# The samples' attention run inside the prompt's attention blocks

## The chip, the cores and the metric

The kernel runs on one core of a Trainium2 chip. The metric is the device time of one execution in microseconds (us). TensorE is called PE below, VectorE DVE, ScalarE ACT, GpSimdE POOL, and SyncE SP.

## What is computed

A two-layer decoder trunk runs one step for a prompt of 1024 tokens and for 8 samples of one token each. Both groups share the weights. Layer 0 has sparse attention with 8 heads of 64 and a retention mixer, layer 1 an SSD mixer, each followed by an MLP. The change concerns the sparse attention alone. An indexer has chosen up to 256 keys for each query. The prompt attends causally to its own keys; each sample attends to 1024 past keys and values, which lie in 8 pages of 128 rows found through a page table, and to its own new key and value:

```python
def sparse_attend(q, kg, vg, idx, tpos, rel_bias):
    dist = tpos[None, :, None] - idx
    bias = jnp.moveaxis(rel_bias[t5_bucket(dist)], -1, 2).astype(jnp.float32)
    logits = jnp.einsum('bqhd,bqkhd->bqhk', q, kg).astype(jnp.float32) * (DH_A ** -0.5) + bias
    logits = jnp.where((dist >= 0)[:, :, None, :], logits, -jnp.inf)
    p = jax.nn.softmax(logits, axis=-1).astype(vg.dtype)
    return jnp.einsum('bqhk,bqkhd->bqhd', p, vg)
```

Keys that were not chosen are masked by a large negative number instead of being gathered out, so that both kernels work on all keys. All of it is fp32.

## The kernel before

The program is a row of stages, each a block of five engine programs that begins when all engines have left the stage before. Inside a stage each engine runs its own list in the order written, and the lists meet through counting semaphores. Around the change the stages are these.

- `project_and_choose` projects to q, k, v and also picks keys for blocks 4 to 6 on DVE.
- `keys_and_values` (L1195) turns k and v into rows on PE, copies them on DVE and stores them from SP's queue. On the same queue a chain of three dependent transfers builds the bias tiles (L1219, L1223, L1226); the stores of k stand behind them.
- `attend` (L1279) is the prompt's attention: 8 blocks of 128 queries, 8 heads in each, 64 steps n in all. Block i sees i+1 tiles of 128 keys. For each step PE makes the logits (`dot`, L1343), turns the probabilities (`turn`, L1353) and multiplies them with the values (`weigh`, L1363). DVE adds mask and bias and takes the row's maximum (`logits`, L1405 to L1414), ACT takes the exponential (L1481) and copies the turned tiles out of PSUM (`copy_turned`, L1473), and POOL prepares the mask with the bias (L1329). PE's list interleaves steps: at an odd n it does the `dot` of n+1 and n+2 first, then `turn(n)`, then `weigh(n-1)`. DVE spends what is left up to block 6 on choosing the keys of block 7 (`choose`, L851 and L853), 64 instructions of 1024 elements spread evenly over the work. After each block its rows are divided by their sums (`rows`, L1423), turned on PE (`turn_rows`, L1372) and split into a high and a low part (`high` on ACT, `low` on DVE) for the output projection.
- `attend_samples` (L1492) follows. SP and POOL load 64 key pages of 256 KB. DVE multiplies each sample's 8 pages by the query that PE has spread over the partitions (L1617) and sums over each head (L1621). A softmax over all samples follows (L1625 to L1651), which goes several times between DVE, PE and ACT. ACT's list holds, ahead of its exponential (L1676), the issues of the value pages of six samples (L1528). PE then multiplies the probabilities, as an 8-column stationary side, with the value pages as moving side, 512 columns each (L1591).
- `retention` comes next.

An fp32 matmul with 128 contraction rows appears in the trace as two records, a transpose as one.

Of the kernel before, what the change touches and what calls it, by code (L numbers as in the profile page):

```python
# [7 lines left out]
F32 = mybir.dt.float32  # L8
F32R = mybir.dt.float32r
I32 = mybir.dt.int32  # L10
ALU = mybir.AluOpType
# [849 lines left out]

def indexer(B, norm):
# [332 lines left out]
def keys_and_values(B):  # L1195
# [17 lines left out]
    with nc.Block() as block:  # L1213
# [27 lines left out]

        @block.tensor
# [36 lines left out]
def attend(B):  # L1279
# [14 lines left out]
    left = B.take("scores_left_sb", [P, NBLK * P])  # L1294
    best = B.take("best_sb", [P, 8])
    s_choice, s_chosen = B.tally("choosing_step"), B.sem("block_chosen")
# [15 lines left out]
    with nc.Block() as block:  # L1312
        @block.gpsimd
# [20 lines left out]
        def _(pe):  # L1334
            def dot(n):
                i, h = seq[n]
                L = width(i)
                if n >= 2:
                    pe.wait_ge(s_log, n - 1)
                r = slice(64 * (h % 2), 64 * (h % 2) + 64)  # L1340
                for c in range(0, L, 512):
                    w = min(512, L - c)
                    ins = nc.tensor.matmul(B.psum[:, 2 * (n % 2) + c // 512, 0:w], B.qkv[r, h // 2, i * P:(i + 1) * P],  # L1343
                                           B.qkv[r, 4 + h // 2, c:c + w], start=True, stop=True)
                ins.then_inc(s_dot, 1)

            def turn(n):
                i, h = seq[n]
                pe.wait_ge(s_prob, n + 1)
                if n >= 1:  # L1350
                    pe.wait_ge(s_pt, n)
                for j in range(i + 1):
                    ins = nc.tensor.transpose(B.psum[:, 4 + j // 4, (j % 4) * P:(j % 4 + 1) * P],  # L1353
                                              logit[:, n % 2, j * P:(j + 1) * P], B.ident[:])
# [12 lines left out]
            def turn_rows(i):  # L1367
                pe.wait_ge(s_o, i + 1)
                if i >= 1:
                    pe.wait_ge(s_lo, i)  # L1370
                for j in range(4):
                    ins = nc.tensor.transpose(B.psum[:, 7, j * P:(j + 1) * P], o[:, j * P:(j + 1) * P], B.ident[:])  # L1372
                ins.then_inc(s_ot, 1)

            dot(0)
            dot(1)
            for n in range(N + 1):
                if n % 2 == 1 and n + 2 < N:
                    dot(n + 1)
                    dot(n + 2)  # L1380
# [4 lines left out]

                if n >= 1 and n % HA == 1 and n > 1:
                    turn_rows(n // HA - 1)
            turn_rows(NBLK - 1)

        @block.vector  # L1390
        def _(dve):
# [25 lines left out]
            def rows(i):  # L1417
                dve.wait_ge(s_pv, HA * (i + 1))
                dve.wait_ge(s_prob, HA * (i + 1))
                if i >= 1:  # L1420
                    dve.wait_ge(s_ot, i)
# [7 lines left out]
            def low(i):  # L1429
                dve.wait_ge(s_hi, i + 1)  # L1430
                out = B.hl[:, 0:4, i * P:(i + 1) * P]
                nc.vector.tensor_tensor(out, B.psum[:, 7, :].rearrange("p (k c) -> p k c", k=4),
                                        B.hh[:, 0:4, i * P:(i + 1) * P].bitcast(F32), ALU.subtract).then_inc(s_lo, 1)

            def choose(step):
                i = LATE + step // (2 * ROUNDS)
                choose_step(dve, s_choice, mask(i), left[:, 0:width(i)], best[:], step % (2 * ROUNDS))
                if step % (2 * ROUNDS) == 2 * ROUNDS - 1:
                    mark_left(dve, s_choice, mask(i), left[:, 0:width(i)])
# [7 lines left out]
            for n in range(N):  # L1447
                logits(n)
                work += width(seq[n][0])
# [5 lines left out]
                if n >= HA and n % HA == 3:  # L1455
                    low(n // HA - 1)
            rows(NBLK - 1)
            low(NBLK - 1)

        @block.scalar  # L1460
        def _(act):
            def high(i):
                act.wait_ge(s_ot, i + 1)
                nc.scalar.copy(B.hh[:, 0:4, i * P:(i + 1) * P],
                               B.psum[:, 7, :].rearrange("p (k c) -> p k c", k=4)).then_inc(s_hi, 1)
# [9 lines left out]
            for n in range(N):  # L1475
# [9 lines left out]
                if n >= HA and n % HA == 2:  # L1485
                    high(n // HA - 1)
            copy_turned(N - 1)
            high(NBLK - 1)
    B.top = mark


def attend_samples(B):  # L1492

    nc = B.nc
    mark = B.top
    KS, VS = 3, 3
    kp = B.take("k_pages_sb", [P, KS, PAGES, 512])
    vp = B.take("v_pages_sb", [P, VS, PAGES, 512])
    pick = B.take("pick_sb", [NS, NS, P])
    maskt = B.take("sample_mask_sb", [P, PAGES, NS])  # L1500
    logit = B.take("sample_logits_sb", [P, NS, PAGES, HA])
    own_prod = B.take("own_product_sb", [NS, 512])
    own = B.take("own_logit_sb", [NS, HA])
    owned = B.take("own_logit_diagonal_sb", [NS, NS, HA])
    pmax = B.take("page_max_sb", [P, NS * HA])
    hmax = B.take("head_max_sb", [NS * HA, 1])
    dmax = B.take("head_max_diagonal_sb", [NS * HA, NS * HA])
    pown = B.take("own_prob_sb", [P, NS * HA])
    pownd = B.take("own_prob_diagonal_sb", [NS, NS, HA])
    den = B.take("denominator_sb", [P, NS * HA])  # L1510
    att = B.take("sample_att_sb", [P, 4, NS])
    kept = pick[:].rearrange("p (s b) c -> p s (b c)", s=2)
    s_kept, s_col = B.sem("own_columns_kept"), B.sem("columns_summed")
    s_k, s_v = [B.sem(f"k_pages_{b}") for b in range(NS)], [B.sem(f"v_pages_{b}") for b in range(NS)]
    s_pick = B.sem("pick_loaded")
    (s_mt, s_q, s_prod, s_dots, s_ob, s_mxt, s_mb, s_sub, s_exp, s_sum, s_pvd, s_fin, s_hi, s_owned, s_pmax,
     s_dmax, s_pownd) = (B.sem(x) for x in (
         "mask_turned", "q_spread", "k_times_q", "dots", "own_spread", "max_turned", "max_spread", "max_subtracted",
         "sample_probs", "probs_summed", "sample_values", "sample_att", "sample_att_high",
         "own_logits", "page_max", "max_diagonal", "own_probs_diagonal"))  # L1520
    s_step = B.tally("sample_step")
    eye8 = B.ident[0:NS, 0:NS].unsqueeze(2).to_broadcast([NS, NS, HA])

    def load(eng, cache, place, b, sem):

        with eng.Fori(0, PAGES) as j:
            page = eng.value_load(B.pages[0:1, bass.ds(j + b * PAGES, 1)], min_val=0, max_val=NPOOL - 1)
            eng.dma_start(place[:, bass.ds(j, 1), :],  # L1528
                          B.i[cache][0][bass.ds(page, 1)].rearrange("o p h d -> p o (h d)")).then_inc(sem, 16)

    def load_keys(eng, parity):
        for b in range(parity, NS, 2):
            if b >= KS:
                eng.wait_ge(s_dots, b - KS + 1)
            load(eng, "cache_k", kp[:, b % KS], b, s_k[b])

    def key_place(b):

        return (NS - KS + b - VS) % KS

    def v_place(b):
        return vp[:, b] if b < VS else kp[:, key_place(b)] if b < VS + KS else vp[:, b - VS - KS]

    with nc.Block() as block:
        @block.sync
        def _(sp):
            sp.dma_start(pick[:].rearrange("p b c -> p (b c)"), B.i["pick"]).then_inc(s_pick, 16)
            load_keys(sp, 0)

        @block.gpsimd  # L1550
        def _(pool):
            load_keys(pool, 1)

        @block.tensor
        def _(pe):
            def to_columns(b):

                pe.wait_ge(s_kept, b + 1)
                for t in range(4):
                    ins = nc.tensor.matmul(B.psum[:, 7, b * 4 + t:b * 4 + t + 1], kept[:, b % 2, t * P:(t + 1) * P],  # L1560
                                           B.ones[0:HA, 0:1], start=True, stop=True)
                ins.then_inc(s_col, 1)

            for j in range(PAGES):
                ins = nc.tensor.transpose(B.psum[:, 0, j * NS:(j + 1) * NS], B.scores_s[:, j * P:(j + 1) * P],
                                          B.ident[0:NS, 0:NS])
            ins.then_inc(s_mt, 1)
            pe.wait_ge(s_pick, 16)
            for b in range(NS):
                if b >= 2:  # L1570
                    pe.wait_ge(s_prod, b - 1)
                nc.tensor.matmul(B.psum[:, 1 + b % 2, :], pick[:, b, :], B.qkv_s[:, 0, :], start=True, stop=True).then_inc(s_q, 1)
            pe.wait_ge(s_owned, 1)
            nc.tensor.matmul(B.psum[:, 3, 0:NS * HA], B.ones[0:NS, :], owned[:].rearrange("p b h -> p (b h)"),
                             start=True, stop=True).then_inc(s_ob, 1)
            pe.wait_ge(s_pmax, 2)
            nc.tensor.transpose(B.psum[0:NS * HA, 4, 0:P], pmax[:], B.ident[:]).then_inc(s_mxt, 1)
            pe.wait_ge(s_dmax, 1)
            nc.tensor.matmul(B.psum[:, 5, 0:NS * HA], B.ones[0:NS * HA, :], dmax[:], start=True, stop=True).then_inc(s_mb, 1)
            pe.wait_ge(s_exp, 2)  # L1580
# [1397 lines left out]
```

## Time and profile before

| | us |
|---|---|
| median of 3 runs | 3987.94 (3981.4 to 4002.66) |
| the profiled execution | 3990.57 |
| its span | 3989.0 |
| PE busy | 3445.2 (86%) |
| DVE busy | 1831.0 (46%) |
| ACT busy | 1086.6 (27%) |
| POOL busy | 1051.1 (26%) |

The span is the time from the first to the last instruction of the profiled execution. Busy time is a sum over the whole program, and a busy PE need not be a fast one: its records grow longer when its clock is lowered. The granted clock, as a share of 2.4 GHz, has two levels here, 1.00 and 0.50 (1.2 GHz); values between them are means over a stretch.

### The profile page before, as it was taken

Reading aid. Unit: us, or ns where it says so; the run is one execution under the profiler, and the core shown is the slowest. Engines: PE = TensorE matmul, PEld = TensorE weight load, DVE = VectorE, ACT = ScalarE, POOL = GpSimd, SP = SyncE. Lnnn points to the kernel's source line nnn. Section 1 sums busy time; section 2 is a strip of 40 time slices with the busy share of each in tenths; the row PEclk is TensorE's granted clock in tenths of the full one; section 3 lists DMA queues with packets and bytes.
Section 4 is the critical chain, followed back from the end, with each engine's and each line's share of the span. In section 5 each row is a group of like instructions: output and inputs, shape, how many; then the busy total and the mean of one; then the engine's idle time right before and its main releaser. Section 6 shows DMA issues by size and latency. Waiting matters only on the chain. (4 is left out here: it accounts for less than half of the span.)

```text
span 3989.0 us, 57770 instructions
## 1 busy us (share of the span) xinstructions
PE 3445.2 (86%) x20584; PEld 3168.3 (79%) x20584; DVE 1831.0 (46%) x3075; ACT 1086.6 (27%) x1873; POOL 1051.1 (26%) x737
## 2 busy tenths in 40 slices
PE   6889968737469999999959988898875999999998
PEld 5439966621359999999948888888865999999998
DVE  3699938761322221212136777777772121212122
ACT  3412204400133221213122444333433231213132
POOL 2002203210213222221124444445443332221222
PEclk8859987858779999999969999999987999999999
DMA  3011230063321111111122222222214111111111
GB/s 115 21 27 47 80 106 1 1 239 99 113 78 47 48 47 48 42 47 48 64 40 73 78 81 86 69 81 64 71 65 152 56 48 48 42 48 47 47 47 65
DMA packets 338555, 261.94 MB, mean 66 GB/s; under 512 B 51646, under 2 KB 307662, under 8 KB 336694
## 3 DMA queue, kind: packets, MB, share of 16 engines
q1 hardware_dynamic: 317174, 208.61, 17.4%
q10 hardware_dynamic: 11520, 25.24, 2.0%
q0 software_dynamic: 9728, 26.47, 1.9%
q8 instruction: 65, 1.06, 0.1%
q14 instruction: 68, 0.56, 0.0%
HBM read 217.36 MB, written 44.74 MB: 66 GB/s over the span
## 5 line engine op out<-in xcount | busy, mean ns | idle before, releaser
L228 POOL TENSOR_TENSOR w_low_sb<-w_loaded_sb,w_high_sb 128x1024 fp32r<-128x1024 f32 (+1 forms) x230 | 555.2, 2414 | 1936.1 <-ACT w_high_sb L222 1924.6
L245 PE MATMUL psum<-act_high_sb,w_high_sb 128*128 128x344 f32 (+1 forms) x2544 | 816.1, 321 | 30.9 <-PEq L186 17.2
L245 PE MATMUL psum<-act_low_sb,w_high_sb 128*128 128x344 f32 (+1 forms) x2544 | 814.4, 320 | 0.0
L245 PE MATMUL psum<-act_high_sb,w_low_sb 128*128 128x344 f32 (+1 forms) x2544 | 814.2, 320 | 0.0
L245 PE MATMUL psum<-second_high_sb,w_high_sb 128*128 128x344 f32 x1704 | 545.5, 320 | 0.0
L245 PE MATMUL psum<-second_low_sb,w_high_sb 128*128 128x344 f32 x1704 | 544.3, 319 | 0.0
L245 PE MATMUL psum<-second_high_sb,w_low_sb 128*128 128x344 f32 x1704 | 544.2, 319 | 0.0
L245 PEld LDWEIGHTS psum<-act_high_sb,w_high_sb 128*128 128x128 f32 (+1 forms) x2544 | 478.3, 188 | 32.6 <-issue 32.3
L245 PEld LDWEIGHTS psum<-act_high_sb,w_low_sb 128*128 128x128 f32 (+1 forms) x2544 | 478.6, 188 | 0.4
L245 PEld LDWEIGHTS psum<-act_low_sb,w_high_sb 128*128 128x128 f32 (+1 forms) x2544 | 478.4, 188 | 0.4
L222 ACT CAST w_high_sb<-w_loaded_sb 128x1024 fp32r<-128x1024 f32 (+1 forms) x230 | 239.5, 1042 | 650.5 <-PE psum L245 601.4
L2423 PE MATMUL psum<-act_high_sb,w_high_sb 128*128 128x344 f32 x1152 | 391.2, 340 | 11.5 <-POOL w_low_sb L228 11.4
L729 DVE TENSOR_TENSOR x_sb<-x_sb,psum 128x344 f32 (+1 forms) x192 | 98.5, 513 | 618.4 <-PE psum L245 618.4
L2423 PE MATMUL psum<-act_low_sb,w_high_sb 128*128 128x344 f32 x1152 | 373.2, 324 | 0.0
L2423 PE MATMUL psum<-act_high_sb,w_low_sb 128*128 128x344 f32 x1152 | 373.0, 324 | 0.0
L245 PEld LDWEIGHTS psum<-second_high_sb,w_low_sb 128*128 128x128 f32 x1704 | 320.3, 188 | 0.0
L245 PEld LDWEIGHTS psum<-second_low_sb,w_high_sb 128*128 128x128 f32 x1704 | 320.0, 188 | 0.0
L245 PEld LDWEIGHTS psum<-second_high_sb,w_high_sb 128*128 128x128 f32 x1704 | 320.0, 188 | 0.0
L2423 PEld LDWEIGHTS psum<-act_high_sb,w_high_sb 128*128 128x128 f32 x1152 | 222.4, 193 | 20.5 <-issue 9.9
L714 DVE SCALAR_TENSOR_TENSOR relu_sb<-psum,rstd_sb 128x344 f32<-128x344 f32 x192 | 99.2, 517 | 294.9 <-PE psum L245 270.8
L2423 PEld LDWEIGHTS psum<-act_low_sb,w_high_sb 128*128 128x128 f32 x1152 | 222.0, 193 | 2.9 <-issue 1.7
L2423 PEld LDWEIGHTS psum<-act_high_sb,w_low_sb 128*128 128x128 f32 x1152 | 221.2, 192 | 0.0
(414 smaller groups left out, 4789.5 us busy)
## 6 DMA issues: line engine op xcount, KB each, us to landing
w_loaded_sb<-in_w_up SPq DMA_DIRECT2D x64, 512.0 KB, 4.0
w_loaded_sb<-in_w_down SPq DMA_DIRECT2D x64, 512.0 KB, 3.6
w_loaded_sb<-in_w_in_odd SPq DMA_DIRECT2D x48, 512.0 KB, 3.9
ecay_sum_spread_sb<-decay_sum_scratch SPq DMA_DIRECT2D x8, 2048.0 KB, 9.7
w_loaded_sb<-in_w_in_even SPq DMA_DIRECT2D x28, 512.0 KB, 3.8
v_pages_sb<-in_cache_v ACTq DMA_DIRECT2D x40, 256.0 KB, 4.3
x_scratch<-x_sb SPq DMA_DIRECT2D x2, 4128.0 KB, 13.9
x_sb<-x_scratch SPq DMA_DIRECT2D x2, 4128.0 KB, 14.9
```

The source lines that it names most:

```text
L222: self.nc.scalar.copy(self.wh[:, par, :, 0:width], self.wf[:, par, :, 0:width]).then_inc(self.s_w_high, 1)
L228: self.nc.gpsimd.tensor_tensor(self.wl[:, par, :, 0:width], self.wf[:, par, :, 0:width], self.wh[:, par, :, 0:width].bitcast(F32), ALU.sub ...
L245: ins = nc.tensor.matmul(out, w[:, par, k, 0:width], a[:, k, cols], start=n == 0, stop=n == 3 * KT - 1)
L714: nc.vector.scalar_tensor_tensor(out=self.relu[:, s, :], in0=B.tile(self.par(e), t), scalar=0.0, in1=self.norm.rstd[:, tcols(t)], op0=ALU.max,
L729: nc.vector.tensor_tensor(xs, xs, B.tile(self.par(e), t), ALU.add).then_inc(B.s_tile_free, 1)
L2423: ins = nc.tensor.matmul(B.psum[:, t, 0:TT], w[:, par(e), k, :], a[:, k, tcols(t)], start=m == 0, stop=m == 3 * KT - 1)
```

## The change

`attend_samples` is removed as a stage. A class `Samples` takes its place and hands pieces of work to the four lists of `attend`, one piece after each step n.

- Page loads. All 128 pages (64 of keys, 64 of values) go through a ring of 7 groups of 4 pages. ACT issues the first 7 groups inside `keys_and_values`; SP issues the other 25 in `attend`, each when its place in the ring is free. POOL loads nothing more.
- Keys, steps 0 to 31 (blocks 0 to 3). In each step PE multiplies two turned key pages, as stationary side in four tiles of 128x128, with two columns that hold the query of one pair of heads, and turns the next two pages (four transposes each). ACT copies each turned page from PSUM.
- Softmax, steps 32 to 38, in small pieces on DVE, PE and ACT.
- Values, steps 38 to 63 without those with n mod 8 of 3 or 4 (20 steps). The value pages are the stationary side, in tiles of 128x128, and the probabilities of two heads the moving side, two columns. There are 32 units of 8 matmuls for the pages and one for the sample's own value.
- `turn_rows`, `high` and `low` are done in two halves at n mod 8 of 3 to 5, with half a PSUM bank, since the samples take the other half. Block 7's keys are chosen in place, without the scratch tile.

The core of the diff:

```diff
+        @block.scalar
+        def _(act):
+            for g in range(smp.RING):
+                smp.load(act, g)
...
+    GROUP = 4
+    RING = 7
+    MAX, SPREAD, SUM = 33, 34, 37
+    VALUES = [n for n in range(38, NBLK * HA) if n % HA not in (3, 4)]
...
+    def turn_pages(self, pe, m):
+        for p in (2 * m, 2 * m + 1):
+            if p % self.GROUP == 0:
+                self.await_group(pe, p // self.GROUP)
+            if p >= 2:
+                pe.wait_ge(self.s_kt, p - 1)
+            for t in range(4):
+                ins = nc.tensor.transpose(B.psum[:, 1 + 2 * (p % 2), t * P:(t + 1) * P], self.page(p)[:, t * P:(t + 1) * P], B.ident[:])
+            ins.then_inc(self.s_kturned, 1)
+    def dot_pages(self, pe, m):
+        for p in (2 * m, 2 * m + 1):
+            pe.wait_ge(self.s_kt, p + 1)
+            for t in range(4):
+                c0 = p * HA + 2 * t
+                ins = nc.tensor.matmul(B.psum[:, 5, c0:c0 + 2], self.kt[:, p % 3, t * P:(t + 1) * P],
+                                       self.qbd[:, t, p // PAGES, :], start=True, stop=True)
...
+    def step_pe(self, pe, n, s_lo):
+        if n < self.TURNS:
+            self.dot_pages(pe, n)
+        if n + 1 < self.TURNS:
+            self.turn_pages(pe, n + 1)
...
+    def weigh_values(self, pe, b, t):
+        out = B.psum[:, 7, c0:c0 + 2]
+        for j in range(PAGES):
+            nc.tensor.matmul(out, self.page(half * self.GROUP + b * PAGES + j)[:, t * P:(t + 1) * P],
+                             self.logit[:, b, j, 2 * t:2 * t + 2], start=j == 0, stop=False)
+        nc.tensor.matmul(out, B.qkv_s[:, 2, t * P:(t + 1) * P], self.pownd[:, b, 2 * t:2 * t + 2],
+                         start=False, stop=True).then_inc(self.s_value, 1)
...
+    def keep_turned(self, act, m):
+        for p in (2 * m, 2 * m + 1):
+            act.wait_ge(self.s_kturned, p + 1)
+            if p >= 3:
+                act.wait_ge(self.s_dots, p - 2)
+            self.B.nc.scalar.copy(self.kt[:, p % 3, :], self.B.psum[:, 1 + 2 * (p % 2), :]).then_inc(self.s_kt, 1)
...
+        @block.sync
+        def _(sp):
+            for g in range(smp.RING, smp.GROUPS):
+                smp.load(sp, g)
...
                 if n >= 1:
                     weigh(n - 1)
-
-                if n >= 1 and n % HA == 1 and n > 1:
-                    turn_rows(n // HA - 1)
-            turn_rows(NBLK - 1)
+                if n >= HA and n % HA in (3, 4):
+                    turn_rows(n // HA - 1, n % HA - 3)
+                if n < N:
+                    smp.step_pe(pe, n, s_lo)
...
-        keys_and_values(B)
-        attend(B)
-        B.top = B.even_top
-        attend_samples(B)
+        smp = Samples(B)
+        keys_and_values(B, smp)
+        attend(B, smp)
```

## Rows read from the trace of the kernel before

**Rows 1.** Page of the profile: granted TensorE clock, in tenths, in 40 slices.

```profile
PEclk8859987858779999999969999999987999999999
```

**Rows 2.** Windows (us from the start): blocks 0-3, block 4, blocks 5-7, samples.

```profile
core 0: us, PE busy (x) PEld busy (x) DVE busy (x) ACT busy (x) POOL busy (x), PEclk, DMA share, GB/s
595.00:661.00 66.00, 52.96 (x258) 39.58 (x259) 49.91 (x154) 28.47 (x89) 23.65 (x35) 0.67 0.00 1
661.00:697.00 36.00, 29.09 (x204) 23.42 (x203) 32.47 (x81) 16.22 (x34) 11.94 (x13) 0.95 0.00 1
697.00:818.00 121.00, 97.05 (x630) 79.14 (x628) 77.18 (x177) 49.00 (x77) 21.16 (x24) 0.86 0.00 1
818.00:1003.00 185.00, 92.63 (x239) 26.04 (x239) 84.75 (x49) 0.99 (x3) 17.43 (x32) 0.70 0.56 182
```

**Rows 3.** Timeline of DVE (start us, length us): last instructions of the two stages.

```profile
817.67 0.69 DVE L1432 TENSOR_TENSOR act_low_sb<-psum,act_high_sb 128x512 fp32r<-128x512 f32 x1 [1.37 <-ACT act_high_sb L1464]
...
1002.38 0.19 DVE L1667 TENSOR_TENSOR act_low_sb<-sample_att_sb,act_high_sb 128x32 fp32r<-128x32 f32 x1 [0.35 <-ACT act_high_sb L1683]
```

**Rows 4.** Groups (busy us, mean ns, idle) of 818 to 1003 us; its softmax window.

```profile
L1591 PE MATMUL psum<-v_pages_sb,sample_logits_sb 128*8 128x512 f32 x80 | 36.2, 606 | 0.0
...
L1617 DVE TENSOR_TENSOR k_pages_sb<-k_pages_sb,psum 128x4096 f32<-128x4096 f32 x8 | 35.3, 4413 | 14.1 <-DMA k_pages_sb<-in_cache_k 14.1
...
906.60:931.10 24.50, 4.81 (x8) 1.39 (x9) 5.91 (x15) 0.78 (x2) 0.00 (x0) 0.50 0.56 160
```

**Rows 5.** Timeline of PE in block 7, clock at 1.0 until 805.

```profile
795.97 1.06 PE L1353 MATMUL psum<-ident_sb,qkv_sb 128*128 128x128 f32 x8 [1.26 <-ACT qkv_sb L1473]
796.87 1.90 PE L1363 MATMUL psum<-v_rows_sb,qkv_sb 128*128 128x64 f32 x16
798.69 1.99 PE L1343 MATMUL psum<-qkv_sb 64*128 64x512 f32 x8
800.62 1.09 PE L1353 MATMUL psum<-ident_sb,qkv_sb 128*128 128x128 f32 x8
...
806.15 3.52 PE L1363 MATMUL psum<-v_rows_sb,qkv_sb 128*128 128x64 f32 x16
```

**Rows 6.** Windows of the line with 17 moving columns (L2137) alone.

```profile
2062.40:2064.70 2.30, 2.30 (x22) 2.30 (x22) 1.00 0.11 25
2064.80:2066.90 2.10, 2.10 (x12) 2.10 (x11) 0.50 0.14 29
```

**Rows 7.** Windows of PE around the one-column matmuls of L780 and L781.

```profile
3969.00:3972.00 3.00, 3.00 (x30) 1.00 0.00 0
3973.00:3974.00 1.00, 1.00 (x7) 0.50 0.00 0
```

**Rows 8.** Windows of PE while it only turns tiles (L1813, L1816).

```profile
1049.00:1054.00 5.00, 4.84 (x22) 0.50 0.00 0
1054.00:1055.00 1.00, 1.00 (x9) 0.80 0.00 0
```

**Rows 9.** Windows inside the attention: 594 to 614, 634 to 654, 660 to 714.

```profile
594.00:614.00 20.00, 14.61 (x61) 10.98 (x62) 12.14 (x45) 7.83 (x32) 8.57 (x16) 0.50 0.00 1
...
634.00:654.00 20.00, 18.33 (x70) 13.61 (x71) 13.67 (x40) 7.43 (x21) 5.98 (x8) 0.51 0.00 1
660.00:714.00 54.00, 42.45 (x304) 34.39 (x304) 49.80 (x121) 24.39 (x51) 15.25 (x18) 0.97 0.00 1
```

**Rows 10.** Groups of 590 to 818.5 us: copy of 128x512 by ACT.

```profile
L1464 ACT CAST act_high_sb<-psum 128x512 fp32r<-128x512 f32 x8 | 4.7, 586 | 6.5 <-PE psum L1372 6.4
```

**Rows 11.** Timeline of SP's and ACT's DMA issues.

```profile
558.57 0.61 SPq L1223 DMA_DIRECT2D bias_rows_scratch<-bias_scratch  x1
567.34 0.39 SPq L1226 DMA_DIRECT2D bias_sb<-bias_rows_scratch  x1
...
892.39 34.01 ACTq L1528 DMA_DIRECT2D k_pages_sb<-in_cache_v  x24
```

**Rows 12.** Window of the stage of the key and value rows.

```profile
552.00:595.00 43.00, 15.60 (x82) 12.29 (x82) 12.74 (x22) 0.00 (x0) 0.00 (x0) 0.67 0.49 162
```

More of the change, by code:

```diff
@@ L859, in mark_left, with choose_in_place @@
     tally.up(dve.scalar_tensor_tensor(out=S, in0=W, scalar=1.0, in1=S, op0=ALU.mult, op1=ALU.is_equal))
+def choose_in_place(dve, tally, S, m8, step):
+    if tally.count:
+        dve.wait_ge(tally.sem, tally.value())
+    tally.up(dve.max(m8, S) if step % 2 == 0 else dve.match_replace(S, m8, S, TAKEN))
 def indexer(B, norm):
@@ L1281, in attend @@
+def attend(B, smp):
     nc = B.nc
@@ L1365, in weigh, with turn_rows @@
                 ins.then_inc(s_pv, 1)
-            def turn_rows(i):
+            def turn_rows(i, half):
                 pe.wait_ge(s_o, i + 1)
[L1369 to L1372, printed above, removed]
+                if half == 1 or i >= 1:
+                    pe.wait_ge(s_lo, 2 * i + half)
+                if half == 0 and i == 0:
+                    pe.wait_ge(smp.s_own, 1)
+                if half == 0 and i == 3:
+                    pe.wait_ge(smp.s_sub, 1)
+                for j in range(2):
+                    c = slice((2 * half + j) * P, (2 * half + j + 1) * P)
+                    ins = nc.tensor.transpose(B.psum[:, 7, j * P:(j + 1) * P], o[:, c], B.ident[:])
                 ins.then_inc(s_ot, 1)
@@ L1376, in _ @@
             dot(1)
+            smp.begin_pe(pe)
             for n in range(N + 1):
-                if n % 2 == 1 and n + 2 < N:
-                    dot(n + 1)
-                    dot(n + 2)
+                if n % 2 == 1:
+                    for m in (n + 1, n + 2):
+                        if m < N:
+                            dot(m)
                 if n < N:
@@ L1454, in _, with high @@
                     rows(n // HA - 1)
-                if n >= HA and n % HA == 3:
-                    low(n // HA - 1)
+                if n >= HA and n % HA in (4, 5):
+                    low(n // HA - 1, n % HA - 4)
             rows(NBLK - 1)
-            low(NBLK - 1)
+            for half in range(2):
+                low(NBLK - 1, half)
+            smp.end_dve(dve)
         @block.scalar
         def _(act):
[L1462 to L1465, printed above, removed]
+            def high(i, half):
+                act.wait_ge(s_ot, 2 * i + half + 1)
+                nc.scalar.copy(B.hh[:, 2 * half:2 * half + 2, i * P:(i + 1) * P],
+                               B.psum[:, 7, 0:256].rearrange("p (k c) -> p k c", k=2)).then_inc(s_hi, 1)
             def copy_turned(n):
@@ L1684, in attend_samples @@
+            for half in range(2):
+                high(NBLK - 1, half)
+            smp.end_act(act)
     B.top = mark
```

399 lines of the change are left out of this document (212 added, 187 removed).

## The prediction

> **What bounds the kernel now.** I read the page's row of the granted clock first [rows 1], then cut the attention and the samples' stage into windows [rows 2]. Most of the kernel is dense matmul at the full clock and is not touched. The samples' stage is 185 us in which no engine works half the time: PE shows 93 us and DVE 85 us, one after the other. DVE's last instruction of the prompt's attention ends at 817.67 + 0.69 = 818.36 and its last of the samples' at 1002.38 + 0.19 = 1002.57 [rows 3], so the stage costs 184 us. Inside it DVE's multiplications of 4.41 us (and reductions as long) bound the keys, the softmax takes 24.5 us though DVE works 5.9 us in it, and PE streams 512 columns per value matmul [rows 4]. The prompt's attention is 223 us. In it PE is busy 80% of each window, and no engine is at its limit for long. Blocks 0 to 3 have a mean clock of 0.67, block 4 of 0.95, blocks 5 to 7 of 0.86 [rows 2].
>
> The question is therefore how much PE work the new form has, and at which clock it runs, since the attention has little idle PE time to hide it in: 66 - 53 = 13 us in blocks 0 to 3 and 121 - 97 = 24 us in blocks 5 to 7 [rows 2].
>
> **Prices on PE, full clock.** In block 7 the eight transposes of a step start at 795.97 and the next group at 796.87: 0.90 us, 0.11 each. The 16 records of `weigh` take 798.69 - 796.87 = 1.82 us, 0.114 each. Two `dot` of 1024 keys take 800.62 - 798.69 = 1.93 us. A step of the prompt with i+1 key tiles thus costs (0.90 + 1.82 + 0.97)/8 = 0.46 us per key tile [rows 5]. The added matmuls with 2 columns have no row of their own. The nearest is L2137, with 128-column weights and 17 moving columns: 22 records under way in 2.30 us, 0.11 each, while the clock is 1.00; 12 in 2.10 us, of which about two lie over the edges, hence 0.21 each, at 0.50 [rows 6]. So fewer columns do not make a record cheaper than 0.11, since the 64-column `weigh` costs the same, and at the low clock all of it doubles: `weigh` goes to 3.52 us for the same 16 records [rows 5].
>
> The Trainium skill, "TensorE: Matmul & The Clock Gate", section LDWEIGHTS, gives a weight load as its columns over 1.2 GHz, about 107 ns for 128 columns, and thus no doubling at the low clock. The 0.21 us above speak against it; by the page the half-clock price of every 2-column record would be halved.
>
> **The change part by part.** All sums are against the profiled execution (span 3989.0, time 3990.57).
>
> 1. Removed: the samples' stage, -184 us.
>
> 2. Keys beside blocks 0 to 3. 64 pages x (4 transposes x 0.11 + 4 matmuls x 2 records x 0.112) = 64 x 1.33 = 85 us on PE. The prompt's own steps are 8 x 0.46 x (1+2+3+4) = 37 us. Together 122 us at the full clock and 244 us at half. ACT copies 64 x 0.586 = 38 us [rows 10] beside its 28 us, far below either, and DVE keeps its 50 us. So PE becomes the bound in place of the exchange between the engines. PE waits in each step for the copy of the pages just turned (0.6 us each), but a step has its own `dot`, `turn` and `weigh` in between, about as long: nothing. The opening work on DVE (a dozen small operations) and three hand-offs in `turn_rows`, whose second half waits within the same step for ACT and DVE, I put at 5 us, together not more than 8.
>
> 3. The clock. In blocks 0 and 1 it was 0.50 for 20 us with PE busy 14.6 us, from 634 to 654 it was 0.51 with PE busy 18.3 of 20 us, and from 660 to 714 it was 0.97 with PE busy 42 of 54 us [rows 9]. So being busy as such does not decide it. The one-column matmuls of L780 and L781 ran back to back at 1.00 from 3969 to 3972, and at 3973 the clock was 0.50 with PE busy all the time [rows 7]; L2137 fell from 1.00 to 0.50 in the middle of its own run [rows 6]. Matmuls of few columns let the clock fall without any idle time. The new form puts 1.8 us of such matmuls into each of the steps 0 to 31 (16 records), and 28.8 records or 3.2 us into each of the 20 value steps. Against that, transposes alone raised the clock: 0.50 from 1049 to 1054, 0.80 in the next us [rows 8], and there are 8 more in each of the steps 0 to 31. I take for blocks 0 to 3 the mean clock that they had, 0.67, as transposes and small matmuls pull both ways: 122/0.67 = 182 us. With the 5 us it is 187 in place of 66: +121. The ends are 122 + 5 - 66 = +61 and 244 + 5 - 66 = +183.
>
> 4. Block 4 (36 us, DVE busy 32 of them [rows 2]). The moved softmax steps are 5.9 us of DVE [rows 4], and DVE is the bound here. For exchanges that now wait within a step I add 3 us. Two value steps add 2 x 3.2 us on PE, of which a part hides; at half clock they are twice that. I take 7. Sum +16, between +9 and +24.
>
> 5. Values beside blocks 5 to 7. 32 units x 9 matmuls x 2 records = 576 records x 0.112 = 64.5 us, of which 18 of 20 steps lie here: 58. The prompt's steps are 8 x 0.46 x (6+7+8) = 77. Together 135 us at full clock, 270 at half. The low stretches of 3.2 us come in three of four steps, nothing raises the clock but the prompt's own work, and the clock was already 0.86 here. I take six tenths of the work at the low level: 135 x 1.6 = 216 us, 3 for hand-offs, against 121: +98. The ends are 135 + 8 - 121 = +22 and 270 + 3 - 121 = +152.
>
> 6. Page loads in `keys_and_values`. 28 pages on ACT's queue, one every 34.01/24 = 1.42 us [rows 11], are 40 us of a stage of 43 us, and ACT is idle there. They move 7.3 MB. The samples' stage moved 182 GB/s at a DMA share of 0.56 [rows 2], 325 GB/s for all queues, so this is 22 us of DMA time in a stage that uses 0.49 of 43 us = 21 us [rows 12]. The sum just fits, but the stage is a chain on SP's queue: the rows of the bias tile take 567.34 - 558.57 = 8.8 us [rows 11], and the bias tile, the stores of k and DVE's copies wait behind them. Each transfer shares the engines with the pages. I take +8, between 0 and +22 (no overlap at all).
>
> 7. SP's 100 page issues in the attention need 100 x 1.42 = 142 us in a stage of over 300, nothing else stands on that queue, and a group is asked for 6 groups (12 steps) ahead: nothing. If that cover went, PE would wait at `await_group` with the turning. POOL loses its issues, which cost nothing. The end work on ACT and DVE: +1.
>
> Sum: -184 + 121 + 16 + 98 + 8 + 1 = +60, so a span of 4049 and a time of 4051. The median stands 2.6 us under the profiled execution: 4048.
>
> **Rivals.**
>
> - The clock holds at 1.00, as it did from 660 to 714 with PE busy 79% [rows 9], because PE is now never idle. Then the sum is -184 + 61 + 9 + 22 + 8 + 1 = -83, a time of 3905: clearly faster. It decides from a mean clock on: all that PE does in blocks 0 to 3 and 5 to 7 is 257 us at full clock, and the change breaks even if these blocks take 66 + 121 + 184 - 16 - 8 - 1 - 8 = 338 us, a mean clock of 0.76. For it speaks that PE's idle gaps go, against it [rows 6, 7]. Chance 0.18; values between it and the forecast are in its lower half.
> - The clock stays low nearly throughout. -184 + 183 + 24 + 152 + 8 + 1 = +184, a time of 4172. For it speaks that from 634 to 654 a busier PE than now did not get it back [rows 9]; against it the transposes [rows 8] and the two steps of each block without values. Chance 0.14.
> - Turning pages does not raise the clock, the rest as forecast: the blocks 0 to 3 are at +183 in place of +121, a time of 4110. [rows 8] speak against it, as nothing but transposes ran there. Chance 0.06. This is what the Trainium skill says in "TensorE: Matmul & The Clock Gate", Part 4, where the full clock "doesn't engage" for transposes; the row differs, and the measurement decides.
> - The transfers bind: pages and bias chain do not overlap, +22 in place of +8, and PE waits for the first groups. A time of 4062 to 4070. Speaks for it the DMA share of 0.9 and over while the bias rows move, against it the sum of item 6. Chance 0.10.
>
> **How the numbers follow.** The forecast, a mixed clock with the time near 4048, has 0.52; its own range, the mean clock of both parts between 0.72 and 0.58, is 4000 to 4100. A measurement of this kernel tells 0.5%, 20 us, from no change: under 3968 is faster, over 4008 slower. The first rival gives 0.18 faster, and the forecast's lower edge 0.02 more. Within 0.5% lie 0.10, from the forecast and the blend with the first rival. The rest, 0.70, is slower. For 8 in 10 the range reaches from 3940 to 4125: it leaves out the first rival's lower half (0.1) and most of the second (0.1).
>
> **What would show it.** In the profile after: the span from the first `logits` to `retention` near 450 us in place of 408; the granted clock of blocks 0 to 3 near 0.67 and of blocks 5 to 7 near 0.62; PE busy over 95% in both, with no engine waited for; 2-column matmuls 0.11 us apart at 1.00 and 0.21 at 0.50; block 4 near 52 us; `keys_and_values` longer by 8 us, its bias rows the longest link. The prediction is wrong if the clock stays at 1.00 through a value step, if PE waits for page copies or page loads, or if the 2-column matmuls are cheaper than the 17-column ones.

## The result and the profile after

| | before | changed |
|---|---|---|
| median, us | 3992.18 (3981.4 to 4002.66, 4 runs) | 4037.43 (4033.08 to 4049.86, 4 runs) |
| ratio to before | | 1.0113, 95% interval 1.0093 to 1.0134 |
| span of the profiled execution, us | 3989.0 | 4048.2 |

The change makes the kernel slower by 45 us; 4048 was forecast, within 3940 to 4125. The profiled execution of the changed kernel is the slowest of its four. One execution of all those in this study, of the form with 16 columns below, took 11795 us; the ratios leave it out, and the median of its other six is 4020.1.

The page's row of the granted clock answers to [rows 1]. A digit is a fortieth of the span, 101 us here. The seventh to the tenth, from 607 to 1012 us, read 5, 8, 5, 6; the same places of the kernel before, samples' stage and all, read 7, 8, 5, 8.

```profile
PEclk8869975856579999999979999999986999999999
```

The windows of the changed kernel answer to [rows 2, 12]. They are cut at the first logits of a block, and the first two windows of [rows 2] are not: at 661 us three of the eight logits of block 3 were still to come. The first logits with block 4's 384 far columns start at 670.00. So the kernel before has to be cut anew, first blocks 0 to 3, then block 4; blocks 5 to 7 are left with 120.3 us, up to 818.

```profile
595.00:671.00 76.00, 62.10 (x314) 46.35 (x315) 57.35 (x174) 32.33 (x98) 27.64 (x39) 0.69 0.00 1
671.00:697.70 26.70, 20.66 (x155) 17.36 (x155) 25.69 (x63) 12.37 (x25) 7.95 (x9) 1.00 0.01 1
```

Of the changed kernel these are the stage of the key and value rows, blocks 0 to 3, block 4, blocks 5 to 7 with the end of the stage. The columns are the time, then busy us and instructions of PE, of its weight loads, of DVE, ACT and POOL, then the clock, the DMA share and GB/s.

```profile
549.50:601.00 51.50, 17.63 (x82) 13.19 (x82) 13.08 (x22) 0.00 (x0) 0.00 (x0) 0.60 0.83 278
601.00:778.00 177.00, 174.52 (x1060) 158.42 (x1060) 60.83 (x187) 67.05 (x165) 27.66 (x39) 0.69 0.31 90
778.00:822.00 44.00, 39.16 (x199) 31.89 (x200) 31.47 (x75) 13.20 (x28) 7.93 (x9) 0.70 0.09 25
822.00:1053.00 231.00, 224.52 (x1191) 201.29 (x1191) 78.68 (x184) 50.01 (x82) 21.17 (x24) 0.63 0.15 42
```

Read the PE column against the time: 174.52 of 177 us and 224.52 of 231 us, at clocks of 0.69 and 0.63. PE is hardly ever free, and it runs at about two thirds of full speed. The 185 us of the samples' window are gone, and 238 us came back elsewhere: +101 in blocks 0 to 3 (177 against 76), +17 in block 4 (44 against 26.7), +111 from block 5 on (231 against 120.3), +8.9 in the stage of the key and value rows (51.5 against 42.6). The cuts are good to about a microsecond. That is +53 in all. Retention begins 50 us later than before, since the stage ahead began 3 us earlier. The rest of the span's difference lies in stages that the diff doesn't touch; from retention to the end they took between 2986 and 3009 us in the profiles of this study. For stretches I therefore use the time from the start of the key and value rows to the start of retention, called the three stages below: 450.6 us before, 503.5 us changed.

PE's waits, grouped by what ended them, from 549 to 1053 us (us in total, times, longest):

```profile
PE psum L1266 <- DVE k_rows_sb L1287: 22.8, 6, 17.5
PE psum L1635 <- PEq L1220: 9.1, 1, 9.1
...
PE psum L1647 <- ACT qkv_sb L1782: 4.7, 5, 2.1
PE psum L1671 <- DVE act_low_sb L1735: 2.6, 3, 1.0
...
PE psum L1635 <- ACT page_turned_sb L1454: 0.8, 1, 0.8
```

The first two belong to the stage ahead and its end. Inside the attention all waits together are some 11 us of 452; turned pages are waited for once, loaded pages never. So exchanges between the engines keep PE waiting for little of the attention, and transfers for none of it. The timeline of PE in two value steps shows what does (start, us, line, columns of the moving side, count):

```profile
902.04 1.81 PE L1441 MATMUL psum<-sample_logits_sb,w_high_sb 128*128 128x2 f32 x8
903.72 1.85 PE L1441 MATMUL psum<-sample_logits_sb,w_low_sb 128*128 128x2 f32 x8
...
916.52 1.00 PE L1441 MATMUL psum<-sample_logits_sb,w_high_sb 128*128 128x2 f32 x8
917.39 1.03 PE L1441 MATMUL psum<-sample_logits_sb,w_low_sb 128*128 128x2 f32 x8
```

Eight records of 2 columns take 903.72 - 902.04 = 1.68 us at the low clock, 0.21 each, and 917.39 - 916.52 = 0.87 us, 0.11 each, at the full one. The price that was taken from a 17-column line [rows 6] is that of 2 columns too.

### The profile page after: what moved, and what is told of

The parts are those of the page before. It is cut to its first block and busy times, and to the rows that moved or that the text cites. A ratio compares the mean times of both kernels' runs of the same rounds, so it can differ in the third digit from the quotient of the medians.

```text
span 4048.2 us, 60149 instructions
## 1 busy us (share of the span) xinstructions
PE 3619.8 (89%) x21704; PEld 3397.2 (84%) x21704; DVE 1758.8 (43%) x3063; ACT 1121.8 (28%) x1945; POOL 1036.3 (26%) x704
## 5 line engine op out<-in xcount | busy, mean ns | idle before, releaser
L245 PE MATMUL psum<-act_high_sb,w_high_sb 128*128 128x344 f32 (+1 forms) x2544 | 817.8, 321 | 31.7 <-PEq L186 17.2
```

The lines of the kernel that those rows point to most:

```text
L245: ins = nc.tensor.matmul(out, w[:, par, k, 0:width], a[:, k, cols], start=n == 0, stop=n == 3 * KT - 1)
```

## The experiments

The theory on record, A: the matmuls of 2 columns keep PE occupied and yet let the granted clock fall, and that is where the gain went. Its rival B: the number of records is what costs, and the clock is that of the prompt's own attention anyhow. Rival C: exchanges between the engines set the pace, and a busy PE is only the look of it.

### The same number of matmuls with wider moving sides

The edit gives each page matmul more columns. The key matmuls of the last 16 pages get fewer than 128, since the PSUM bank ends (`min(128, 512 - c0)`). The extra columns multiply data that happens to stand beside, and their products are written over by later matmuls or never read.

```diff
-        self.logit = B.take("sample_logits_sb", [P, NS, PAGES, HA])
+        self.flat = B.take("sample_logits_sb", [P, NS * PAGES * HA + 128])
+        self.logit = self.flat[:, 0:NS * PAGES * HA].rearrange("p (b g h) -> p b g h", b=NS, g=PAGES)
...
-        c0 = 448 + b * HA + 2 * t
-        out = B.psum[:, 7, c0:c0 + 2]
+        c0 = 320 + b * HA + 2 * t
+        out = B.psum[:, 7, c0:c0 + 128]
         for j in range(PAGES):
+            o = (b * PAGES + j) * HA + 2 * t
             nc.tensor.matmul(out, self.page(half * self.GROUP + b * PAGES + j)[:, t * P:(t + 1) * P],
-                             self.logit[:, b, j, 2 * t:2 * t + 2], start=j == 0, stop=False)
+                             self.flat[:, o:o + 128], start=j == 0, stop=False)
...
-                ins = nc.tensor.matmul(B.psum[:, 5, c0:c0 + 2], self.kt[:, p % 3, t * P:(t + 1) * P],
-                                       self.qbd[:, t, p // PAGES, :], start=True, stop=True)
+                w, o = min(128, 512 - c0), (t * NS + p // PAGES) * 2
+                ins = nc.tensor.matmul(B.psum[:, 5, c0:c0 + w], self.kt[:, p % 3, t * P:(t + 1) * P],
+                                       self.qflat[:, o:o + w], start=True, stop=True)
```

Both sides:

> The edit: every page matmul of the samples (keys and values) gets 128 moving columns in place of 2; the 126 extra columns are overwritten by later matmuls or never read, so the count of records stays 512 + 512. Theory A (the narrow matmuls let the granted clock fall, and the low clock is what the attention stage pays): a record of 128 moving columns costs about what a 2-column one costs at the full clock (0.11 us, as the transposes of 128 columns), the clock stays near 1.00, blocks 0 to 3 fall from 177 to 122-135 us, block 4 from 44 to 38-42, blocks 5 to 7 from 230 to 135-150: the kernel near 3905 (3885 to 3935), faster than both. Theory B (the time is set by the number of records, and the low clock belongs to the prompt's own attention, whose clock was 0.67 and 0.86 before): blocks 0 to 3 stay at 170-180 us, 5 to 7 at 220-240, the kernel at 4030 to 4060. Theory C (exchanges between the engines pace it, PE only looks busy): clock up, but the stretches stay above 165 and 215 us.

Keys alone:

> The edit: 128 moving columns for the key pages alone (steps 0 to 31), values as in the changed kernel. A: blocks 0 to 3 at 122-135 us with a clock over 0.9, blocks 5 to 7 unchanged at 230: 3990 (3980 to 4000), no longer told from the kernel before. B: 4030 to 4050.

Values alone:

> The edit: 128 moving columns for the value pages alone (steps 38 to 63), keys as in the changed kernel. A: blocks 5 to 7 at 135-150 us with a clock over 0.9, blocks 0 to 3 unchanged at 177: 3952 (3940 to 3970). B: 4030 to 4050.

The control with 16 columns:

> The edit: 16 moving columns for keys and values, a control: it changes the same lines as the 128-column form and writes extra columns too, but the matmuls stay narrow. A: the clock of the two stretches stays within 0.05 of the changed kernel's (0.69 and 0.63), the kernel at 4037 within 15 us. If it is as fast as the 128-column form, something else in the edit (the order of writes, the place of the results) makes the gain, and A falls. B: 4037 too.

| | median, us | ratio to before, 95% | blocks 0-3, us (clock) | block 4 | blocks 5-7 |
|---|---|---|---|---|---|
| changed, 2 columns | 4037.4 | 1.0113 (1.0093 to 1.0134) | 177 (0.69) | 44 (0.70) | 231 (0.63) |
| 128, keys and values | 3926.6 | 0.9828 (0.9803 to 0.9852) | 133 (0.98) | 40 (0.66) | 157 (0.99) |
| 128, keys alone | 4000.6 | 1.0015 (1.0000 to 1.0031) | 134.5 (0.97) | 41.5 (0.63) | 233.5 (0.62) |
| 128, values alone | 3978.9 | 0.9949 (0.9929 to 0.9969) | 173 (0.72) | 40.5 (0.66) | 157 (0.99) |
| 16, keys and values | 4024.8 | 1.0083 (1.0047 to 1.0118) | 153 (0.82) | 41.7 (0.63) | 230 (0.63) |

Windows of the form with 128 columns for both (blocks 0 to 3, block 4, blocks 5 to 7), and of the control with 16 (the same three):

```profile
601.80:735.00 133.20, 130.05 (x1074) 118.85 (x1075) 61.77 (x191) 65.28 (x165) 27.74 (x39) 0.98 0.40 121
735.00:775.00 40.00, 38.05 (x197) 31.70 (x197) 32.11 (x77) 13.28 (x28) 7.99 (x10) 0.66 0.07 21
775.00:932.30 157.30, 149.75 (x1180) 132.39 (x1179) 77.39 (x180) 50.03 (x82) 21.20 (x24) 0.99 0.21 61
```

```profile
602.00:755.00 153.00, 150.28 (x1072) 136.86 (x1072) 61.86 (x192) 66.09 (x165) 27.66 (x39) 0.82 0.37 107
755.00:796.70 41.70, 39.82 (x196) 32.60 (x195) 31.82 (x77) 13.27 (x28) 7.94 (x9) 0.63 0.05 16
796.70:1027.00 230.30, 223.78 (x1184) 200.23 (x1183) 77.61 (x180) 50.31 (x82) 21.16 (x24) 0.63 0.14 42
```

The count of PE's records is the same in every row of the table but for records missing from the traces (1074, 1072 and 1060 in blocks 0 to 3), and so are pages, copies, waits and transfers. With up to 64 times the columns in each page matmul the kernel is 111 us shorter than the changed one, and 1.7% under the kernel before. Each half of the edit acts only in its own stretch, 177 to 134.5 and 231 to 157 (the other half's stretch stays at 173 and 233.5), and the shares add up: the three stages are 503.5 us (changed), 463.5 (keys), 423 (values) and 383 (both), which is -40, -80 and -121. B is refuted, and C too: the exchanges are there as before.

Three expectations were clearly off, and the keys alone came out just above their range (4000.6, 3980 to 4000). Blocks 5 to 7 took 157 us, where A gave 135 to 150. A value unit (eight page matmuls and the own value, 18 records) takes 2.25 us at the full clock, 0.125 per record with its two small ones, as the timeline of that form shows, where 18 x 0.112 = 2.0 was reckoned; 31 of the 32 units lie in this stretch, and not 28.8; and waits, the turned rows and the end of the stage come on top.

```profile
809.01 1.11 PE L1445 MATMUL psum<-sample_logits_sb,act_low_sb 128*128 128x128 f32 x8
809.96 1.06 PE L1445 MATMUL psum<-sample_logits_sb,w_loaded_sb 128*128 128x128 f32 x8
810.95 0.38 PE L1447 MATMUL psum<-wn_prob_diagonal_sb,sample_qkv_rows_sb 8*128 8x2 f32 x2
811.26 0.87 PE L1652 MATMUL psum<-ident_sb,qkv_sb 128*128 128x128 f32 x6
```

The values alone gave 3979, not 3952: its three stages are 80 us shorter than the changed kernel's (423 against 503.5), but its untouched stages were the longest of all in that profile (3009 us, 13 more than in the changed kernel's). Why they were is not shown; its ten executions spread from 3957 to 3989. And the control with 16 columns is not neutral: in blocks 0 to 3, where 8 transposes of 128 columns stand between the narrow matmuls, the clock rose from 0.69 to 0.82; in blocks 5 to 7 it stayed at 0.63. Its kernel time can't be told from the changed kernel's (the intervals overlap). The gain thus does not come from the new place of the results, which the control has too, and it depends on the columns by degrees.

### Idle matmuls in the kernel before

The smallest test has nothing of the change in it: at the head of steps 0 to 31 of the kernel before stand 8 matmuls whose products nobody reads, of 2 columns or of 128.

```diff
             for n in range(N + 1):
+                if n < 4 * HA:
+                    for _ in range(8):
+                        nc.tensor.matmul(B.psum[:, 5, 0:2], B.ident[:], B.ident[:, 0:2], start=True, stop=True)
                 if n % 2 == 1 and n + 2 < N:
```

> The kernel before with nothing of the change in it but 8 idle matmuls of 2 moving columns (16 records, into a PSUM bank that is free there) at the head of each of the steps 0 to 31: the smallest test of the clock without pages, copies, transfers or waits. PE's own work in blocks 0 to 3 is 37 us at the full clock, the idle matmuls add 512 x 0.112 = 57, together 94. Theory A (narrow matmuls let the clock fall): a clock of 0.50 to 0.65 and 145 to 190 us in place of 76 (first product to the first logits of block 4), the kernel 70 to 110 us slower than before. Theory B (only the number of records counts, the clock stays at what the prompt's own work had, 0.70): 115 to 135 us, the kernel 40 to 60 us slower.

> The same with 128 moving columns in the idle matmuls. A: the clock rises above 0.9 and the stretch takes 94 to 110 us, 20 to 35 us over before, and 40 us or more below the narrow twin, though each matmul does 64 times the work. B: the same time as the narrow twin or longer.

Measured: 4092.3 us with 2 columns (ratio 1.0233, 1.0203 to 1.0262) and 4020.3 with 128 (1.0057, 1.0032 to 1.0083). Windows from the first product to the first logits of block 4, the narrow form first:

```profile
591.70:764.60 172.90, 172.90 (x822) 158.37 (x823) 57.88 (x175) 33.41 (x98) 27.61 (x39) 0.53 0.00 1
```

```profile
592.50:693.70 101.20, 101.20 (x828) 91.57 (x828) 57.69 (x176) 32.24 (x98) 27.62 (x39) 0.98 0.00 1
```

In the kernel before this stretch is 76 us. By the profile PE is busy for the whole of both windows, with the same records. 172.9 x 0.53 = 92 and 101.2 x 0.98 = 99: the same work, at two clocks (94 had been reckoned). Here there are no pages, no copies and no transfers, so the fall of the clock belongs to the narrow matmuls themselves. The Trainium skill ("TensorE: Matmul & The Clock Gate", section "HAM oscillation — how this bites in real kernels") has as its rule that gaps in PE's work are what brings the clock down. In the narrow form the profile shows no gap at all, and the clock is 0.53. By that rule it would have been 1.00, and the stretch 92 us long, 80 us shorter, by an estimate from the window above. For PE's distance from its limit the Trainium skill ("Perfetto Trace Analysis", section "Identifying the Most-Contended Engine") gives two measures, the floating point work against the peak and the busy share of the weight loads. The second doesn't show the loss here: weight loads are busy 158.37 of 172.9 us, 92%, at about half the pace that PE could have. The clock beside it does.

This pair also bears on the prediction's third rival, by which turning pages does not raise the clock. The narrow form has 16 narrow records per step and no pages to turn, and its clock is 0.53; the changed kernel has as many with 8 transposes beside them, and its clock is 0.69.

### Fewer records

> Leaves out three of four key matmuls of each page (only the last pair of heads has logits) and seven of eight page matmuls of each value unit; transposes, copies, transfers and softmax steps stay. Records fall by 384 in blocks 0 to 3 and by 448 from step 38 on, at the full clock 43 and 50 us, at the low clock twice that. A: blocks 0 to 3 at 90 to 115 us (79 at full clock), blocks 5 to 7 at 120 to 145 (as in the kernel before plus the hand-offs), the kernel near 3870 (3840 to 3900). C (exchanges pace it): still over 150 and 190 us.

```diff
-            for t in range(4):
+            for t in (3,):
                 c0 = p * HA + 2 * t
...
-        for j in range(PAGES):
+        for j in range(1):
             nc.tensor.matmul(out, self.page(half * self.GROUP + b * PAGES + j)[:, t * P:(t + 1) * P],
```

3877.9 us (0.9697, 0.9667 to 0.9727). Its windows of blocks 0 to 3 and 5 to 7:

```profile
605.30:711.00 105.70, 100.12 (x705) 86.37 (x706) 61.46 (x191) 65.12 (x165) 27.68 (x39) 0.85 0.54 153
...
749.40:890.60 141.20, 125.69 (x750) 106.70 (x749) 77.17 (x180) 49.64 (x82) 21.16 (x24) 0.76 0.24 68
```

Without three quarters of the key matmuls and seven eighths of the page matmuls for the values, and with all turns, copies, softmax steps and transfers kept, 177 us become 106 and 231 become 141. C is out once more. It also shows how little the full count costs at the full clock: blocks 5 to 7 took 157 us with all matmuls at 128 columns, 16 us more than here without 448 of the records.

### The page loads ahead of the attention

```diff
-            for g in range(smp.RING):
+            for g in range(2):
                 smp.load(act, g)
...
-            for g in range(smp.RING, smp.GROUPS):
+            for g in range(2, smp.GROUPS):
                 smp.load(sp, g)
```

> The changed kernel, but ACT issues only 2 of the 7 page groups in the stage of the key and value rows; SP issues the other 5 at the head of the attention. If the page transfers are what lengthened that stage by 9 us (51.6 against 42.7), it is back at 43 to 46 us, and the attention, whose PE is never kept waiting for a page group, stays at 452 us: 4030 (4022 to 4036). If it was something else (a slower clock in that stage, the turns on PE), it stays at 51 us. If SP then falls behind in the first steps, PE waits at the first groups and the attention grows by 3 us or more.

The stage of the key and value rows took 46.1 us in place of 51.5. The kernel's time didn't move, where 4030 had been expected: 4039.6 us, ratio 1.0108 (1.0083 to 1.0132), with an interval wider than the 5 us in question. SP's issues in the stage, the changed kernel first, then this one, then the stores of k in the kernel before, name the place:

```profile
556.40 0.62 SPq L1230 DMA_DIRECT2D bias_rows_scratch<-bias_scratch  x1
564.78 0.39 SPq L1233 DMA_DIRECT2D bias_sb<-bias_rows_scratch  x1
565.22 21.70 SPq L1238 DMA_DIRECT2D out_k_prompt<-k_rows_sb  x8
```

```profile
555.37 0.61 SPq L1230 DMA_DIRECT2D bias_rows_scratch<-bias_scratch  x1
564.62 0.39 SPq L1233 DMA_DIRECT2D bias_sb<-bias_rows_scratch  x1
565.05 15.27 SPq L1238 DMA_DIRECT2D out_k_prompt<-k_rows_sb  x8
```

```profile
567.77 13.72 SPq L1231 DMA_DIRECT2D out_k_prompt<-k_rows_sb  x8
```

The bias rows take 8.4 and 9.3 us here against 8.8 before [rows 11]: the 7.3 MB of pages don't hold them up. It is the eight stores of k behind them that stretch, from 13.72 us before and 15.27 here to 21.70 us with all the pages under way. DVE, whose copies need the buffers that these stores free, waits for them 17.2 us before, 19.6 here and 25.4 in the changed kernel.

### The low clock of block 4

At 128 columns one low stretch was left, around block 4. Three forms add idle matmuls of 128 columns there: in step 31 alone, the same with the late page loads, and in steps 31 to 33 with the late loads. The second part of the diff is in the last alone (and in the form with 64 columns below):

```diff
+            if m == self.TURNS - 1:
+                for _ in range(8 // 2):
+                    nc.tensor.matmul(B.psum[:, 7, 256:384], B.ident[:], B.ident[:], start=True, stop=True)
             ins.then_inc(self.s_dots, 1)
...
+        if n in (self.TURNS, self.MAX):
+            for _ in range(8):
+                nc.tensor.matmul(B.psum[:, 7, 256:384], B.ident[:], B.ident[:], start=True, stop=True)
```

> The 128-column form had the low clock from about 737 to 765 us, at the entry of block 4: step 31 has key matmuls cut to 62 columns and less (the bank ends), no pages to turn after them, and PE waits 0.95 us for the scaled page logits. Here 8 idle matmuls of 128 columns stand among those of step 31 (+16 records, 1.8 us). If a short stretch of narrow work is what drops the clock, and the prompt's own steps then can't raise it for 28 us: the clock stays at 1.00 through block 4, which falls from 39.6 to 25-32 us, the kernel 6 to 12 us below the 128-column form: 3917 (3912 to 3922). If the clock falls anyway (block 4's own work is too thin after the wait), it is 1 to 3 us slower: 3928.

> The same with only 2 of the 7 page groups loaded in the stage of the key and value rows. The stage at 43 to 46 us in place of 52, the rest as its twin: another -5 to -9 us, near 3910. The steps are shorter here (4 us against 5.5), so SP's 1.4 us per page is closer to what two pages per step need (2.8 us): if PE waits for page groups in blocks 0 to 3, the gain is lost.

> With idle matmuls in step 31 alone the clock fell all the same, 6 us later (about 743 us), behind a wait of 1.89 us for DVE in step 32, and came back at 764. Here steps 32 and 33 have 8 idle matmuls of 128 columns each as well (16 records, 1.8 us, each). If the thin PE work of these steps is what drops the clock, it stays at 1.00 through block 4, which goes from 40 to 28-34 us: the kernel at 3912 (3907 to 3916), against 3921 for its twin. If it falls at another step of block 4, or DVE's softmax steps set the pace of block 4 whatever the clock is, the stretch stays at 38-42 us: 3921 to 3925.

Block 4 of the form with one filled step, then of that with three:

```profile
728.90:768.90 40.00, 36.90 (x210) 31.42 (x209) 31.69 (x74) 13.27 (x28) 7.95 (x9) 0.74 0.07 21
```

```profile
730.60:770.40 39.80, 36.77 (x241) 30.90 (x241) 31.63 (x74) 13.20 (x28) 7.95 (x9) 0.87 0.07 21
```

The key matmuls of step 31 have 16 columns and fewer, not the 62 of the expectation. The clock of block 4 went from 0.66 over 0.74 to 0.87, and the block took 40 us each time. The expected 6 to 12 us did not come. DVE is busy 32 of the 40 us in all of them, and its waits for results of PE are most of the rest: 6.7 us in the plain form, 7.1 with three filled steps. The fill is not free either: PE has 241 records there in place of 197, stays busy for 37 us, and part of the fill stands ahead of results that DVE waits for. So a clock raised by idle matmuls bought nothing here. What a higher clock would bring without them is not shown by these forms. The kernel before gives a hint: its block 4, without any idle matmuls, took 28.4 us at a clock of 0.79 behind the narrow ones of blocks 0 to 3, and 26.6 us at 1.00 behind the wide ones. The medians: 3925.8 us with one filled step, 3921.0 with the late loads besides (0.9822, 0.9799 to 0.9845; near 3910 was expected), 3922.2 with three filled steps (0.9814, 0.9801 to 0.9828). Between these and the plain form with 128 columns nothing can be told at the kernel's level; in the profiles the three stages are 383 us (plain), 383, 377 and 378, so the late loads keep their 5 us and PE never waits for a page there either.

> The same with 64 moving columns in the samples' matmuls (the idle ones keep 128). A record of 64 costs what one of 2 or of 128 costs at the full clock (0.11 us). The question is whether 64 columns keep the clock up as the prompt's own matmuls of 64 columns among wider ones do. If they keep it, the time is its twin's within 5 us. If each fall of the clock is now slower to mend, or 64 are too few, blocks 0 to 3 and 5 to 7 lie 5 to 40 us above the twin's 133 and 157.

With 64 columns the clock is 0.94 and 0.98 where its twin had 0.97 and 0.99, blocks 0 to 3 take 136 us (twin 134), blocks 5 to 7 156 (twin 157). The kernel has 3926.8 us (0.9822, 0.9801 to 0.9843): 64 columns do here what 128 do.

## Why the prediction was right

| step of the prediction | forecast, us | measured, us |
|---|---|---|
| samples' stage | -184 | -184 |
| blocks 0 to 3 | +121, to 187 (clock 0.67) | +101, to 177 (clock 0.69) |
| block 4 | +16, to 52 | +17, to 44 |
| blocks 5 to 7, with the end | +99 (clock near 0.62) | +111 (clock 0.63) |
| key and value rows | +8 | +8.9 |
| sum | +60 | +53 in the stages, 45 in the medians |

The mechanism was right: PE becomes the bound, and matmuls of 2 columns keep it at a low clock. That the sum came so close is in part luck, since errors of 10 us and more stand against each other in it.

- The base of the first two rows was misread. The 66 us of "blocks 0 to 3" in [rows 2] lack the last ten of block 3, and the 36 us of "block 4" hold them. The 187 us were worked out for all of blocks 0 to 3, and the 52 us kept the end of block 3 in block 4: 10 us were counted twice. Without them the prediction's own prices give +111, +16 and a sum of +50.
- The price of a 2-column record, taken from 17 columns, held at both clocks: 0.11 to 0.12 and 0.21 to 0.22 us. So it does double at the low clock. With it the PE work of blocks 0 to 3 was 122 us at the full clock, and 122/0.69 = 177 is the window. The 5 us for hand-offs did not come on top; PE's waits there are 2.4 us.
- The clock was the one open quantity, and both values came out within 0.02. That was partly luck for blocks 0 to 3: 0.67 was carried over from the kernel before, where another mixture gave it, and from a window with the wrong end (with the right one it is 0.69). The value isn't sharp either: with the same key matmuls it was 0.72 in the profiles of the late loads and of the values alone. What was sound in it is the cause, matmuls of few columns, read from two lines far from the change [rows 6, 7], and the counterweight of the transposes [rows 8]. The pairs of 2 and 128 columns show the first directly. The second is borne out, not isolated: the clock is 0.53 with narrow matmuls and no page transposes, 0.69 with them.
- Block 4 grew as forecast, once its base is right. DVE's work went from 25.7 to 31.5 us, 5.8 for the 5.9 of the softmax steps. "DVE is the bound here" holds for most of the block but not for its end. There DVE waits for PE behind the one value unit of the window and a `dot`, both at the low clock, 5.44 us, and 0.53 in the form with 128 columns:

```profile
821.94 0.69 DVE L1708 CUSTOM_DVE_ANT_0 qkv_sb<-psum,scores_sb 128x512 f32<-128x512 f32 x1 [5.44 <-PE psum L1635]
773.65 0.69 DVE L1713 CUSTOM_DVE_ANT_0 qkv_sb<-psum,scores_sb 128x512 f32<-128x512 f32 x1 [0.53 <-PE psum L1640]
```

- Blocks 5 to 7 were put too low by 12 us. PE was busy 224.5 us at 0.63, 141 us at the full clock, against 135. By their start on PE 31 of the 32 value units lie behind the first logits of block 5, not 18/20 of them: 2.2 units of 18 records, 4.4 us. The 16 transposes of the turned rows, 1.8 us, weren't counted. At the low clock a unit took 906.01 - 902.04 = 3.97 us, as priced (36 x 0.112 = 4.03). PE's idle time, most of it at the end of the stage, is 6.5 us against 3.
- The key and value rows: the size was right, the place half so. The bias chain is a long link but didn't grow; the stores of k behind it did.
- PE waits for the copy of a turned page once, for 0.8 us, and never for a load: item 7 and "nothing" in item 2 held.
- The first rival, the clock at 1.00, was not what this kernel does, but it was priced well: nearly forced by wide moving sides (0.98 and 0.99), the kernel takes 3927 us where that sum gave 3905. What it missed is mostly in blocks 5 to 7 (+37 measured, +22 reckoned). The second and third rival have blocks 0 to 3 at about 249 us, and they took 177. The fourth, transfers that keep PE waiting, did not occur.

The chance of 0.18 on a clock that holds rested on PE having no idle gaps any more. The idle matmuls in the kernel before show that this alone does not hold the clock: at 100% busy it was 0.53.

## What to carry to other kernels

Before work is moved beside other work on PE, price it in records times the time of a record at the clock that the mixture will have, not in busy share: fp32 matmuls of 2 columns cost as much here as those of 64 or 128 at the full clock, and they nearly halved the clock for everything around them. Where such matmuls can't be avoided and PE is the bound, widen their moving side into columns that nobody reads; here that turned a loss of 1.1% into a gain of 1.7%, with no instruction added to the attention but a few to prepare the tiles. Look first whether PE is the bound: in block 4, where DVE is busy four fifths of the time, a clock raised with idle matmuls was worth nothing. And cut the windows of both kernels at the same instruction before you subtract them; a cut ten microseconds off counted the same work twice here.

## What the runs showed of the hardware

- 64 times the columns in less time: 512 idle records of 2 columns stretched 76 us to 173, and of 128 columns to 101. A record of fp32 with 128 rows and 128 columns of weights took 0.11 us at the full clock for 2, 64 and, within a tenth, 128 moving columns.
- A PE that is 100% busy, and whose weight loads are busy 92%, ran at a mean clock of 0.53.
- The clock answers by degrees: with 2, 16, 64 and 128 columns in the key matmuls it was 0.69, 0.82, 0.94 and 0.98 in blocks 0 to 3. In the value steps, without transposes of pages, 16 columns gained nothing (0.63) and 64 nearly all (0.98). The form with 64 had the late loads and the filled steps as well. Widths between 16 and 64 were not tried. With 2 columns the 0.69 was 0.72 in two other forms.
